# Long depthwise convolution of the last branch: eight taps on TensorE, and its layer norm by column sums

## What is computed

```python
h = _rmsnorm(x, odd_norm)
proj = h @ w_in                       # 1024 -> 3072: val, gate, z
g = val * sigmoid(gt)
c = depthwise causal conv of g over time, 31 taps per channel, + conv_b
mu = mean(c over the 1024 channels);  cc = c - mu
c = cc * rsqrt(mean(cc * cc) + 1e-5) * ln_g + ln_b
y = silu(c) * silu(z)
x = x + y @ w_out                     # then the final rms norm
```

## Time and profile before

| | us |
|---|---|
| median of 3 runs (2700.43 to 2708.34) | 2705.96 |
| the profiled execution, whole | 2705.07 |
| its span in the trace | 2703.0 |
| PE busy, of the span | 2543.4 (94%) |
| POOL busy | 1306.4 (48%) |
| DVE busy | 1021.1 (38%) |
| ACT busy | 994.2 (37%) |

### The profile page before, as it was taken

How to read it: one execution, slowest core, us unless ns; L and a number is a source line. 1 busy time by engine, 2 the same in 40 slices (tenths; PEclk the granted TensorE clock), 3 DMA queues, 4 the chain that set the end, 5 groups by cost and what they waited for, 6 DMA issues and landing times. The chain is left out here.

```text
span 2703.0 us, 31611 instructions
## 1 busy us (share of the span) xinstructions
PE 2543.4 (94%) x11308; PEld 2058.7 (76%) x11308; DVE 1021.1 (38%) x1557; ACT 994.2 (37%) x1340; POOL 1306.4 (48%) x686
## 2 busy tenths in 40 slices
PE   8999999999999999999999999999999986887877
PEld 6888878756888888888887776788888875776656
DVE  3223330054622211522214612553223179244973
ACT  5333323276533333433333333353333332233452
POOL 5555545300565554655544433245555462357843
PEclk9999989999999999999998998899999988999898
DMA  3333333200233233223332321023233322322211
GB/s 139 94 95 118 125 104 97 90 1 16 78 93 101 93 101 109 78 93 101 94 109 71 100 78 55 1 78 106 96 94 100 109 88 61 84 78 71 62 54 63
DMA packets 69331, 228.34 MB, mean 84 GB/s; under 512 B 8803, under 2 KB 13283, under 8 KB 69132
## 3 DMA queue, kind: packets, MB, share of 16 engines
q1 hardware_dynamic: 63456, 218.63, 25.3%
q10 hardware_dynamic: 4956, 5.61, 0.8%
q0 software_dynamic: 848, 3.15, 0.3%
HBM read 222.75 MB, written 6.84 MB: 85 GB/s over the span
## 5 line engine op out<-in xcount | busy, mean ns | idle before, releaser
L370 POOL TENSOR_TENSOR wl_sb<-raw_sb,wh_sb 128x1024 fp32r<-128x1024 f32 x401 | 975.8, 2436 | 1042.0 <-ACT wh_sb L362 1039.5
L1698 PE MATMUL banks<-xh_sb,wh_sb 128*128 128x512 f32 x2064 | 814.8, 395 | 49.4 <-POOL wl_sb L370 42.2
L1700 PE MATMUL banks<-xl_sb,wh_sb 128*128 128x512 f32 x2064 | 810.2, 393 | 0.0
L1699 PE MATMUL banks<-xh_sb,wl_sb 128*128 128x512 f32 x2064 | 810.1, 393 | 0.0
L362 ACT ACTIVATE wh_sb<-raw_sb 128x1024 fp32r<-128x1024 f32 x401 | 423.9, 1059 | 732.1 <-DMA raw_sb<-weights 728.1
L1698 PEld LDWEIGHTS banks<-xh_sb,wh_sb 128*128 128x128 f32 x2064 | 392.3, 190 | 139.0 <-issue 42.4
L1699 PEld LDWEIGHTS banks<-xh_sb,wl_sb 128*128 128x128 f32 x2064 | 392.7, 190 | 81.2
L1700 PEld LDWEIGHTS banks<-xl_sb,wh_sb 128*128 128x128 f32 x2064 | 391.6, 190 | 82.3
L1698 PE MATMUL banks<-hh_sb,wh_sb 128*128 128x512 f32 x704 | 273.9, 389 | 0.0
L1699 PE MATMUL banks<-hh_sb,wl_sb 128*128 128x512 f32 x704 | 273.9, 389 | 0.0
L1700 PE MATMUL banks<-hl_sb,wh_sb 128*128 128x512 f32 x704 | 273.9, 389 | 0.0
(11 more groups left out here) (367 smaller groups left out, 2706.3 us busy)
## 6 DMA issues: line engine op xcount, KB each, us to landing
raw_sb<-weights SPq DMA_DIRECT2D x404, 512.0 KB, 3.5
scratch<-scratch ACTq DMA_DIRECT2D x1, 2560.0 KB, 11.7
x_sb<-x_in SPq DMA_DIRECT2D x8, 256.0 KB, 8.6
mix_sb<-scratch POOLq DMA_DIRECT2D x1, 2048.0 KB, 8.9
out<-hf_sb SPq DMA_DIRECT2D x8, 256.0 KB, 2.2
turn<-mix_sb SPq DMA_DIRECT2D x4, 256.0 KB, 4.7
mix_sb<-turn SPq DMA_DIRECT2D x4, 256.0 KB, 4.7
turn<-mix_sb ACTq DMA_DIRECT2D x4, 256.0 KB, 2.7
```

Source lines behind the costliest of these rows:

```text
L370: pool.tensor_tensor(wl[:, slot, :], raw[:, slot, :], wh_f[:, slot, :], ALU.subtract).then_inc(w_split, 1)
L1698: pe.matmul(dst, wh[:, q, cols], in_hi, start=first, stop=False)
L1699: pe.matmul(dst, wl[:, q, cols], in_hi, start=False, stop=False)
L1700: return pe.matmul(dst, wh[:, q, cols], in_lo, start=False, stop=last)
```

## The change

The 31 taps are divided anew: 8 on PE, 19 on DVE, 4 on ACT and POOL. For PE's eight (taps 0 to 7), SP writes each finished chunk of g to DRAM (`park`) and reads it back four times, each copy a token later and on 32 partitions, so that one partition axis holds 4 shifts of 32 channels (`shifted`). POOL makes small matrices with the tap weights on four stacked diagonals (`weights_of_taps`), and PE does eight float32 matmuls of 128 rows by 32 columns per chunk, on four column tiles of the array (`conv_taps`). ACT moves the result with the bias to SBUF and POOL adds it to its own sum. The blocks of `odd.in` come in another order (ODD: three z blocks stand between the gates, five at the end), all loops of the branch are written out, and DVE works on two chunks half a chunk apart. POOL also adds the eight chunks up (`add_total`), so that one matmul with ones gives the mean; PE does it ahead of the last block. The variance goes by `col_sum`, the root and reciprocal by 128 by 4 values and `spread_rate`; ACT loads the tables of Sqrt and Silu ahead of their use by activations on one column, and alternates silu and high part. The rest of the diff only declares semaphores, an event, 64 columns of weights and a stacked identity, and puts the blocks in DRAM in the new order.

```diff
-POOL_TAPS = 7
...
+TAPS_PE, TAPS_DVE, TAPS_POOL = 8, 19, 4
+ROWS_TAP = 32
...
+ODD, _of = [], {"v": 0, "g": 0, "z": 0}
+for _kind in "vgvgvgvgzvgvgzvgvgzzzzzz":
+    ODD.append((_kind, _of[_kind]))
+    _of[_kind] += 1
+GATE_AT = {c: b for b, (kind, c) in enumerate(ODD) if kind == "g"}
...
+total = region(16896, T)
 tap_acc = sig_o
+taps = [[region(17408 + T * (TAPS_POOL * q + j), T) for j in range(TAPS_POOL)] for q in range(2)]
+pe_sum = [rstd[:, :], acc[:, :]]
+LONG = T + 4
+moved = [buf.rearrange("p (q n) -> p q n", n=LONG) for buf in (region(21504, 4 * LONG), hf_f[:, 0:4 * LONG])]
+tap_mat = [hf_f[:, 4 * LONG + 512 * q:4 * LONG + 512 * (q + 1)].rearrange("p (s n) -> p s n", n=ROWS_TAP)
+           for q in range(2)]
...
+WIDE = LONG + 3
+def parked(c):
+    return bass.AP(tensor=scratch.tensor, offset=scratch.offset + P * WIDE * c, ap=[[WIDE, P], [1, WIDE]])
+def park(sp, c):
+    sp.wait_ge(g_mul, c + 1)
+    sp.dma_start(parked(c), gpad[:, c, 0:WIDE]).then_inc(g_parked, 16)
+def shifted(sp, c):
+    sp.wait_ge(g_parked, 16 * (c + 1))
+    if c >= 2:
+        sp.wait_ge(pe_taps, c - 1)
+    for j in range(4):
+        sp.dma_start(moved[c % 2][ROWS_TAP * j:ROWS_TAP * (j + 1), :, :],
+                     parked(c)[:, j:j + LONG].rearrange("(q c) n -> c q n", c=ROWS_TAP)
+                     ).then_inc(g_moved[c % 2], 16)
+def odd_in_tensor(pe, first_three):
+    def conv_taps(c):
+        pe.wait_ge(g_moved[c % 2], 64 * (c // 2 + 1))
+        pe.wait_ge(tap_weights, c // 2 + 1)
+        if c >= 2:
+            pe.wait_ge(pe_kept, c - 1)
+        for a in range(TAPS_PE // 4):
+            for q in range(4):
+                last = pe.matmul(banks[ROWS_TAP * q:ROWS_TAP * (q + 1), 6 + c % 2, :],
+                                 tap_mat[c // 2 % 2][:, 8 * (c % 2) + 2 * q + a, :],
+                                 moved[c % 2][:, q, 4 * a:4 * a + T], start=(a == 0), stop=(a == 1),
+                                 tile_position=(0, ROWS_TAP * q))
+        last.then_inc(pe_taps, 1)
...
+    for b in range(3, len(ODD)):
+        if b == len(ODD) - 1:
+            pe.wait_ge(o_total, KD - 1)
+            pe.matmul(banks[:, 6, :], ones, total, start=True, stop=True).then_inc(o_sum, 1)
+        pe.wait_ge(w_split, BLK["odd.in"] + b + 1)
+        if b >= 4:
+            pe.wait_ge(tiles_freed, FREE0 + TILE["odd.in"] + b - 3)
+        block_mm(pe, lin[b % 4], b % 4, xh, xl)
+        for c in range(KD):
+            if b == GATE_AT[c] + (3 if c else 4):
+                conv_taps(c)
 
 def odd_tensor(pe):
+    event = EVENT["odd.ln"]
     for c in range(KD):
+        pe.wait_ge(squares, c + 1)
+        mm = col_sum(pe, sums[1], gpad[:, c, 0:T], c == 0, c == KD - 1)
+    mm.then_inc(cols_summed, 1)
+    spread_rate(pe, event, diag_post, 7)
...
+    def tap_products(c):
+        act.wait_ge(g_mul, c + 1)
+        if c >= 2:
+            act.wait_ge(tap_sum[c % 2], TAPS_POOL * (c // 2) - 1)
+        for j in range(TAPS_POOL):
+            tap = CONV_K - TAPS_POOL + j
+            act.activation(taps[c % 2][j], gpad[:, c, tap:tap + T], ACT.Copy,
+                           scale=conv_weight(c, tap)).then_inc(tap_prod, 1)
+    def keep_pe_sum(c):
+        act.wait_ge(pe_taps, c + 1)
+        if c >= 2:
+            act.wait_ge(tap_sum[c % 2], TAPS_POOL * (c // 2))
+        bias = VEC["conv_b"] + c
+        act.activation(pe_sum[c % 2], banks[:, 6 + c % 2, :], ACT.Identity,
+                       bias=vec[:, bias:bias + 1]).then_inc(pe_kept, 1)
+    for b, (kind, c) in enumerate(ODD):
+        if b:
+            high_part(act, "odd.in", b % 4, b - b % 4)
+        for other in range(KD):
+            if b == GATE_AT[other] + 1:
+                tap_products(other)
+            if b == GATE_AT[other] + (4 if other else 5):
+                keep_pe_sum(other)
+        if b == len(ODD) - 1:
+            for other in range(KD):
+                act.wait_ge(o_cen, other + 1)
+                act.activation(gpad[:, other, 0:T], cc[:, other, :], ACT.Square).then_inc(squares, 1)
+        act.wait_ge(blocks_done, BLK["odd.in"] + b + 1)
+        if kind == "g":
+            act.activation(gpad[:, c, PAD:PAD + T], lin[(b - 1) % 4], ACT.Copy)
+            act.activation(sig_o[:, c, :], lin[b % 4], ACT.Sigmoid).then_inc(tiles_freed, 2)
+        if kind == "z":
+            act.activation(zz[:, c, :], lin[b % 4], ACT.Silu).then_inc(tiles_freed, 1)
+    act.activation(unused(), inv_d, ACT.Sqrt)
+    act.wait_ge(cols_summed, EVENT["odd.ln"] + 1)
+    act.activation(root, sums[1], ACT.Sqrt, bias=eps[:, 1:2]).then_inc(root_ready, 1)
+    act.activation(unused(), inv_d, ACT.Silu)
+    for c in range(KD + 1):
+        if c < KD:
+            act.wait_ge(o_n, c + 1)
+            b = VEC["ln_b"] + c
+            act.activation(cc[:, c, :], cc[:, c, :], ACT.Silu, bias=vec[:, b:b + 1]).then_inc(o_s, 1)
+        if c:
+            act.wait_ge(t_ready, TNO["odd.y"] + c)
+            act.activation(xh[:, c - 1, :], hf[:, c - 1, :], ACT.Copy).then_inc(hi_ready, 1)
...
+    half = (TAPS_DVE + 1) // 2
+    def tap_step(c, n):
+        s, tap = c % 2, TAPS_PE + n
+        if n == TAPS_DVE:
+            dve.wait_ge(o_tap[s], done[s])
+            dve.wait_ge(tap_sum[s], TAPS_POOL * (c // 2 + 1))
+            tt(cc[:, c, :], conv_bank(c), tap_acc[:, c, :], ALU.add).then_inc(o_conv, 1)
+            return
+        g = gpad[:, c, tap:tap + T]
+        if n == 0:
+            dve.wait_ge(g_mul, c + 1)
+            if c >= 2:
+                dve.wait_ge(o_conv, c - 1)
+            ins = ts(conv_bank(c), g, conv_weight(c, tap), None, ALU.mult)
+        else:
+            dve.wait_ge(o_tap[s], done[s])
+            ins = stt(conv_bank(c), g, conv_weight(c, tap), conv_bank(c), ALU.mult, ALU.add)
+        ins.then_inc(o_tap[s], 1)
...
+        done[s] += 1
+    for c in range(KD + 1):
+        for n in range(half):
+            if c > 0:
+                tap_step(c - 1, half + n)
+            if c < KD:
+                tap_step(c, n)
     dve.wait_ge(o_sum, 1)
     for c in range(KD):
+        stt(cc[:, c, :], banks[:, 6, :], -1.0 / D, cc[:, c, :], ALU.mult, ALU.add).then_inc(o_cen, 1)
+    event = EVENT["odd.ln"]
+    rate_vector(dve, event, rate_post, diag_post)
+    dve.wait_ge(spread, event + 1)
+    for c in range(KD + 1):
+        if c < KD:
+            b = VEC["ln_g"] + c
+            dve.wait_ge(squares, c + 1)
+            stt(cc[:, c, :], cc[:, c, :], vec[:, b:b + 1], banks[:, 7, :], ALU.mult, ALU.mult).then_inc(o_n, 1)
+        if c:
+            dve.wait_ge(o_s, c)
+            tt(hf[:, c - 1, :], cc[:, c - 1, :], zz[:, c - 1, :], ALU.mult).then_inc(t_ready, 1)
...
-    loads(first + 12, BLOCKS)
+    loads(first + 12, BLK["odd.in"])
+    for b in range(len(ODD)):
+        some([BLK["odd.in"] + b])
+        if b >= 5 and ODD[b - 5][0] == "g":
+            shifted(sp, ODD[b - 5][1])
+        if b >= 4 and ODD[b - 4][0] == "g":
+            park(sp, ODD[b - 4][1])
+    loads(BLK["odd.out"], BLOCKS)
...
+    def weights_of_taps(i):
+        if i >= 2:
+            pool.wait_ge(pe_taps, 2 * i - 2)
+        col = VEC["tap_w"] + 16 * i
+        shape = [P, 16, ROWS_TAP]
+        pool.tensor_tensor(tap_mat[i % 2], cst_sb[:, C_STACK:C_STACK + ROWS_TAP].unsqueeze(1).to_broadcast(shape),
+                           vec[:, col:col + 16].unsqueeze(2).to_broadcast(shape),
+                           ALU.mult).then_inc(tap_weights, 1)
+    def add_tap(c, j):
+        a, before = tap_acc[:, c, :], TAPS_POOL * (c // 2)
+        pool.wait_ge(tap_prod, TAPS_POOL * c + j + 1)
+        if j > 1:
+            pool.wait_ge(tap_sum[c % 2], before + j - 1)
+        pool.tensor_tensor(a, taps[c % 2][0] if j == 1 else a, taps[c % 2][j],
+                           ALU.add).then_inc(tap_sum[c % 2], 1)
+    TOTAL_AT = {11: 1, 14: 2, 16: 3, 19: 4, 21: 5}
+    def add_total(c):
+        pool.wait_ge(o_conv, c + 1)
+        if c > 1:
+            pool.wait_ge(o_total, c - 1)
+        pool.tensor_tensor(total, cc[:, 0, :] if c == 1 else total, cc[:, c, :], ALU.add).then_inc(o_total, 1)
+    def add_pe_sum(c):
+        a = tap_acc[:, c, :]
+        pool.wait_ge(pe_kept, c + 1)
+        pool.wait_ge(tap_sum[c % 2], TAPS_POOL * (c // 2) + TAPS_POOL - 1)
+        pool.tensor_tensor(a, a, pe_sum[c % 2], ALU.add).then_inc(tap_sum[c % 2], 1)
+    for b, (kind, c) in enumerate(ODD):
+        if b:
+            low_part(pool, "odd.in", b % 4, b - b % 4)
+        if kind == "v" and c % 2 == 0:
+            weights_of_taps(c // 2)
+        for other in range(KD):
+            if b == GATE_AT[other] + 1:
+                add_tap(other, 1)
+                add_tap(other, 2)
+            if b == GATE_AT[other] + 2:
+                add_tap(other, 3)
+            if b == GATE_AT[other] + (4 if other else 5):
+                add_pe_sum(other)
+        if kind == "g":
+            gated(b, c)
+        if b in TOTAL_AT:
+            add_total(TOTAL_AT[b])
+    for c in range(len(TOTAL_AT) + 1, KD):
```

(25 more changed lines are left out.)

127 lines of the change are left out of this document (24 added, 103 removed).

## The result

The changed kernel took **2675.55 us**, the median of 4 runs (2672.3 to 2682.02), beside 2704.35 (2700.43 to 2708.34) for the one before on the same chip: a ratio of 0.9896, 95% interval 0.9875 to 0.9916. The forecast was 2682, in a range of 2668 to 2698. The profiled execution took 2682.02 us, span 2680.3.

The account below looks back on a forecast made before the run. PE, busy 94% of the span, was taken as the bound, with gains where it waits; 11.3 (to block 23's end) + 10.1 (norm) + 2.4 (hand-over) = 23.8 us off 2705.07 gave 2681.3, median 2682, range 2668 to 2698.

Parts of the forecast that it names:

- Part 1: Blocks 3 to 22 of odd.in: PE's 31.4 us of waits for POOL's low parts go; DVE's last chunk complete near 2574.
- rival 4: DVE stays behind PE, its chain ending 10 us later than 2574: 2685 or so; chance within the remaining 0.03.
- Part 2: Taps on PE: eight float32 matmuls on four concurrent column tiles take 2.0 us a chunk, 16 us for eight chunks.
- the right rival: Taps on PE: column tiles of one bank don't run together, 6.9 us a chunk, 2718 us; chance 0.08, half-way 0.06.
- Part 3: Copies of g through DRAM just fit, 15 against 16.3 us; chunks 0 and 1 late; block 22 ends at 2579.7.
- rival 2: Copies through DRAM come late, PE waiting for DMA ahead of the taps: up to 14 us, 2696; chance 0.13.
- Part 4: Ahead of block 23 PE idles 10.1 us for the total; ones and block 23 take 9.1; 11.3 us gained.
- rival 3: Ahead of block 23 the total is in time: 10.1 idle and 2.8 of low clock saved, 2669; chance 0.10.
- Part 5: Layer norm: column sums 11 us, root to spreading 3.0, then 2.9; 16.9 us in place of 27.0, 10.1 gained.
- Part 6: Hand-over to odd.out: products and low parts take turns, first three blocks 19.1 us where now 21.5, 2.4 gained.
- The sum: Whole kernel: 11.3 + 10.1 + 2.4 = 23.8 us off 2705.07, 2681.3; 2682 us as median; forecast's chance 0.60.
- the rest: Stretch from 2658.7 on, after the first three blocks of odd.out: 44.3 us that the change touches nothing of.

Follow-up runs that it names:

- experiment 4: Changed kernel with tap matmuls ordered tile by tile: 2679.04 us; a second kernel with all eight on one column tile: 2715.71 us.
- experiment 9: Changed kernel with the write of g to DRAM and the four reads each issued one block later: 2712.24 us.
- experiment 1: Changed kernel with the total's adds of chunks 5, 6 and 7 in POOL's turn 21, ahead of the late low parts: 2662.63 us.
- experiment 3: Kernel before, old taps and block order, with variance by column sums and silu alternating with high part: 2699.7 us.
- experiment 2: Changed kernel's taps and block order with the layer norm of the kernel before: 2679.42 us.
- experiment 7: On experiment 1, POOL adds squares in pairs, four column sums for eight: 2663.35 us; also with chunk 1's taps one block later: 2663.26.
- experiment 8: On experiment 7's second kernel, squares and pairs go ahead of block 26's high and low parts: 2656.61 us; chunks 2, 3 later too: 2656.45.
- experiment 5: Changed kernel without the two activations that preload the Sqrt and Silu tables: 2678.94 us.

## Why the prediction was right, step by step

**Part 1 held.** The waits for low parts went, from 31.4 us to 1.4 in `odd.in`. DVE ended at 2579.4 against my 2574, from a start 4.2 us later, and nobody waited for it: rival 4 is out. Against the 17 us of low clock in the earlier trace rows the window is at 1.00.

**Part 2 held**, and experiment 4 shows the concurrency to be what decides: with it the change gains, without it the whole is 2715.7. It was the right rival to name, at the right price (2718). The group of taps takes 1.85 us; with the change of tile shape, which my 2.0 were to include, it is 2.1: the groups of chunks 2 and 3 start at 2494.26 and 2507.26, 13.0 us apart with two blocks of 5.44 between. That is 1 us more over eight chunks than I had.

**Part 3 held in sum, and partly by luck.** I had 1.6 us of lateness for chunk 0 and 2.6 for chunk 1; measured were 0.5, seen only on PE's weight loads, and 3.7, so both were wrong and their sum of 4.2 was right. The 2.0 us of low clock behind these waits did not come. Block 22 ended 150.6 us into the stage, forecast 151.4: that agreement is made of errors of either sign. What I got wrong is rival 2. "Up to 14 us" was built from lateness alone; experiment 9 shows that one block's delay costs 36.9, because the lateness comes back in every chunk, and PE's clock fell behind these waits.

**Part 4 held to 0.3 us**: 9.8 us idle for 10.1, and 9.3 for ones and block 23, forecast 9.1. The reading that gave it, POOL's order against SP's wait for block 22, is shown by experiment 1, which is rival 3 made true: 2662.6 where I wrote 2669. The changed kernel itself was 6 us below my forecast too, and the difference of the two, 12.9 us, is what I had put on this wait and its clock.

**Part 5 held**: 10.4 us of column sums for 11, then 6.0 as forecast, 16.3 for 16.9. The clock fell in the middle of the column sums, as it had in the middle of 16 in the earlier trace rows: 64 instructions took 10.4, 10.7 and 12.5 us in the changed kernel and experiments 1 and 3, in experiment 1 with no wait ahead of them.

**Part 6 was mis-sized**: 18.2 us for 19.1, so 3.3 gained for 2.4. In the old norm of experiment 2 the 4.60 us of the earlier trace rows came back, and the first three blocks took 21.2; with the old taps and the new order, in experiment 3, they took 18.0. So the order of products and low parts is what counts. In the changed kernel DVE's products beside the low parts are lengthened, from the second on:

```profile
2618.42 0.68 DVE L1708 TENSOR_TENSOR hf_sb<-mix_sb 128x512 f32<-128x512 f32 x1
2619.02 0.74 DVE L1705 SCALAR_TENSOR_TENSOR mix_sb<-mix_sb,vecs_sb,banks 128x512 f32<-128x512 f32 x1
2619.68 1.12 DVE L1708 TENSOR_TENSOR hf_sb<-mix_sb 128x512 f32<-128x512 f32 x1
```

A product of two SBUF inputs takes 1.12 us there for 0.68; L1705, with one input in PSUM, is not touched (0.74). The Trainium skill, SBUF — State Buffer, section "SBUF: two separate sides", says that of a GpSimd instruction and a DVE instruction with two SBUF inputs, whichever starts first has the shared port pair for its whole length and the other blocks. The trace agrees: the low part took 4.60 us where a run of products had begun before it (2635.82 and 2637.25), and the product of 1.12 us began at 2619.68, behind the start of a low part at 2618.59.

**The sum.** 11.3 + 10.1 + 2.4 = 23.8 was forecast. Block 23 ended 169.8 us into the stage; before it was 181.9 (2610.2 less 2428.31), so 12.1. Norm 10.7, first three 3.3, and 0.8 in the rest, which I had called untouched: 26.9. No step failed. Four sums were a little cautious, and inside the first the single terms were off by up to 2 us and made up for each other. The 0.8 in the rest, and some of the 3.3, are within what a stage wanders. The medians differ by 28.8, of which some 2 us are within what a start that wanders does to a few runs.

**Left open.** Why the start of the stage differs by up to 6.7 us between executions with the same code ahead. Why PE's clock fell behind a wait of 3.6 us in experiment 4 and not behind one of 3.7 us in the changed kernel.

## What to carry to other kernels

When a piece of work is moved ahead of a barrier, look for every instruction that stands before it in the same engine's stream, and ask what each of those waits for: here a weight block for the next projection, released by the very block that was meant to hide the wait. The mistake is as easy to make again in the repair (experiment 7) as it was in the change, and it can cost twice, as PE's clock fell with the idle time: 9.8 us of wait and 3.0 us of slow matmuls here. And price a late transfer by how often it comes back and what the engine's clock does behind it, not by its lateness alone. And look at the clock inside a run of small matmuls too: right behind a full block, 64 column sums took 10.7 us and 32 took 3.7, because the clock fell while the 64 ran.

## What the runs showed of the hardware

- Eight float32 matmuls of 128 by 32 on four column tiles: 1.85 us, 3.8 times as fast as on one tile (6.98); tile by tile instead of round the tiles it was 1.87.
- A column sum instruction (128 by 128 with one column, float32) takes 0.116 us at the full clock (experiment 8) and, on average over runs that were mostly at the low one, 0.195 to 0.198 (experiments 3 and 7). 64 of them took 10.7 us right behind a full block with no wait (experiment 1): the clock fell from 1.00 to 0.50 while they ran. 32 took 3.7 us right behind a full block (experiment 8) and 6.35 behind 2.0 us of idle time (experiment 7).
- A load of a table does not wait for what its activation waits for: it ended 8.4 us ahead (experiment 5).
- Behind waits of PE of 3.6 to 4.4 us a group of taps took 3.31 to 3.64 us for 1.85, at the low clock in whole or in part (experiments 4 and 9); behind one of 3.7 us in the changed kernel it took 1.93.
- The slowest of four reads of 258 KB, issued 0.4 us behind a load of 512 KB on the same queue, landed 7.3 to 8.0 us after issue in experiment 9, 7.4 and 8.2 in the changed kernel, and 5.6 to 6.8 there where no load stood so close ahead. The write of 260 KB to DRAM took 2.9 us at the median in the changed kernel and 4.7 in experiment 9; the earlier trace rows have 4.7 for four that came together.
